# Second expert stage: 32 more tokens gathered instead of multiplied, v split and waited for in halves

## The reference, cut to what matters

```python
q = (xt @ w_query).reshape(n, PEER_HEADS, 2, PEER_DKEY // 2)
s = jnp.einsum('nhmd,mkd->nhmk', q, sub_keys).astype(jnp.float32)
sv, si = lax.top_k(s, PEER_TOPK)
...
fv, fpos = lax.top_k(cand, PEER_TOPK)
eidx = jnp.take_along_axis(cidx, fpos, axis=-1)
gate = jax.nn.softmax(fv, axis=-1).astype(h.dtype)
...
act = jax.nn.gelu(jnp.einsum('nd,nhkd->nhk', x_blk, expert_u[i_blk]))
return jnp.einsum('nhk,nhkd->nd', g_blk * act, expert_v[i_blk])
```

## Time and profile before

| | us |
|---|---|
| median of 3 runs | 4635.27 (4634.18 to 4642.76) |
| profiled execution | 4642.33, span 4640.6 |
| TensorE busy in the span | 4358.9 (94%) |
| second expert stage, first matmul to last add | 3298.1 to 4382.9 |
| TensorE busy in it (L2774) | 1074.2 for 6144 matmuls |
| mean granted TensorE clock | 0.971 |

### The profile page before, as it was taken

One profiled execution on the slowest core, in us unless ns is written; L12 is line 12 of the kernel. 1 busy time (PEld: TensorE's weight loads), 2 busy tenths in 40 slices (PEclk: granted clock), 3 DMA queues, 4 the chain that ended last, 5 costly groups with the idle time before them and its releaser, 6 DMA issues. The chain is left out here.

```text
span 4640.6 us, 80519 instructions
## 1 busy us (share of the span) xinstructions
PE 4358.9 (94%) x29764; PEld 4156.5 (90%) x29764; DVE 2641.2 (57%) x4339; ACT 1537.7 (33%) x2344; POOL 2535.1 (55%) x1826
## 2 busy tenths in 40 slices
PE   7899976999998898999999999999899999999999
PEld 5788875888787897999999999999899999999899
DVE  4477764554434302679566666655576767767621
ACT  3122213443443323223333333333333333333232
POOL 5687751322222342445566666657566666666543
PEclk9999987999999998999999999999899999999999
DMA  4233322334984532333589999979888888878533
GB/s 113 71 94 93 94 62 89 104 100 125 375 316 148 192 111 75 99 92 129 199 314 340 328 344 323 346 256 332 306 323 328 336 331 320 340 281 335 210 97 95
DMA packets 365052, 993.54 MB, mean 214 GB/s; under 512 B 43922, under 2 KB 121490, under 8 KB 305970
## 3 DMA queue, kind: packets, MB, share of 16 engines
q1 hardware_dynamic: 268370, 554.21, 36.1%
q0 software_dynamic: 46560, 337.14, 18.7%
q10 hardware_dynamic: 49920, 99.47, 5.6%
HBM read 904.93 MB, written 85.72 MB: 213 GB/s over the span
## 5 line engine op out<-in xcount | busy, mean ns | idle before, releaser
L2774 PE MATMUL val_y_ps<-val_wt,val_v 128*128 128x384 f32 x6144 | 1074.2, 335 | 30.4 <-DVE val_wt L2848 23.7
L2774 PEld LDWEIGHTS val_y_ps<-val_wt,val_v 128*128 128x128 f32 x6144 | 1068.0, 188 | 36.1 <-issue 31.4
L248 PE MATMUL rt_acc<-xn_act,rt_w_hi 128*128 128x384 f32 x4096 | 1062.8, 340 | 31.0 <-POOL rt_w_rest L238 30.7
L238 POOL TENSOR_TENSOR rt_w_rest<-rt_w_raw,rt_w_hi 128x512 fp32r<-128x512 f32 x576 | 736.9, 1304 | 509.5 <-ACT rt_w_hi L233 507.2
L248 PEld LDWEIGHTS rt_acc<-xn_act,rt_w_hi 128*128 128x128 f32 x4096 | 739.1, 188 | 46.3 <-POOL rt_w_rest L238 42.6
L2736 POOL TENSOR_TENSOR val_v<-val_v_raw,val_v 128x2048 fp32r<-128x2048 f32 x128 | 591.0, 4617 | 327.1 <-ACT val_v L2807 327.0
L248 PE MATMUL rt_acc<-xn_act,rt_w_rest 128*128 128x384 f32 x2048 | 691.8, 338 | 0.0
L2651 DVE CUSTOM_DVE_ANT_0 rt_space<-rt_space,rt_mid 128x2048 f32<-128x2048 f32 x160 | 360.9, 2280 | 216.1 <-DMA rt_space<-in_peer_u,out_row_id 208.5
L2869 DVE TENSOR_TENSOR out_xT<-out_xT,val_y_ps 128x384 f32<-128x384 f32 x512 | 282.3, 551 | 339.6 <-PE val_y_ps L2774 339.4
L233 ACT ACTIVATE rt_w_hi<-rt_w_raw 128x512 fp32r<-128x512 f32 x576 | 334.6, 627 | 283.3 <-PE rt_acc L248 196.7
L248 PEld LDWEIGHTS rt_acc<-xn_act,rt_w_rest 128*128 128x128 f32 x2048 | 383.7, 187 | 0.0
(11 more groups left out here) (428 smaller groups left out, 7308.8 us busy)
## 6 DMA issues: line engine op xcount, KB each, us to landing
rt_w_raw<-in_peer_uT SPq DMA_DIRECT2D x512, 256.0 KB, 5.2
val_v_raw<-in_peer_vp SPq DMA_DIRECT2D x128, 1024.0 KB, 5.0
scan_w_raw<-in_w_in SPq DMA_DIRECT2D x128, 256.0 KB, 3.2
att_w_raw<-in_w_in SPq DMA_DIRECT2D x96, 256.0 KB, 3.4
hid_scratch<-rt_hid ACTq DMA_DIRECT2D x128, 192.0 KB, 6.2
gate_scratch<-rt_space ACTq DMA_DIRECT2D x12, 2048.0 KB, 10.3
val_hid<-hid_scratch SPq DMA_DIRECT2D x32, 768.0 KB, 8.3
val_gate<-gate_scratch SPq DMA_DIRECT2D x32, 768.0 KB, 11.5
```

Source lines behind the costliest of these rows:

```text
L238: e.tensor_tensor(self.rest[:, s, 0:nk, :], self.raw[:, r, 0:nk, :], self.hi[:, s, 0:nk, :].bitcast(F32), ALU.subtract).then_inc(self.rest ...
L248: mm = e.matmul(acc[:, h, 0:width], w[:, s, k, :], act[:, kt0 + k, a, col + h * width:col + (h + 1) * width], start=first and k == 0 and w ...
L2774: mm = e.matmul(y_ps[:, t % 2, 0:DW], v[:, c % 2, a, j, t * P:(t + 1) * P], wt[:, g % 2, j, b, :], start=j == 0 and a == 0 and b == 0, sto ...
```

## The change

32 of the dense tokens, 160 to 191, become gathered tokens: `V0` = 192 is the first dense token of the second stage, `VTOK` = 352 their number, and 32 more gathers (`NV` = 192) bring their v rows. Their hidden values are still made by the dense product of the first stage; 32 single-element gathers (`picked`) fetch from `hid_scratch` what each of their picks needs. The gate table has 11 chunks. `v` and `v_rest` are handled in two halves of 256 columns: rounding, remainder and TensorE's wait are per half, and the gathers stand between the two remainders of a chunk. There are five row buffers, three turns of rows (`SETS`, `TURNS`), and the last set of rows ends one chunk ahead of the stage's end.

```diff
-ROWS, VROWS = 3, 4
+NV = NR + XK
+V0 = D0 + EX
+VTOK = TOK - V0
+ROWS, VROWS = 3, 5
...
-        NCH = DTOK // CH
+        NCH = VTOK // CH
...
             e.wait_ge(ids_ready, 1)
-            for g in range(P // EX):
-                r, c = slice(g * EX, (g + 1) * EX), slice(g * XK, (g + 1) * XK)
-                e.dma_start(k.row_id[r, HK:NR], more_id[:, c]).then_inc(more_in, 16)
-                e.dma_start(k.row_gate[r, HK:NR], more_gate[:, c]).then_inc(more_in, 16)
+            def spread(m):
+
+                picks, toks = slice(HK + m * XK, HK + (m + 1) * XK), slice(m * EX, (m + 1) * EX)
+                for g in range(P // EX):
+                    r, c = slice(g * EX, (g + 1) * EX), slice(g * XK, (g + 1) * XK)
+                    e.dma_start(k.row_id[r, picks], more_id[toks, c]).then_inc(more_in, 16)
+                    e.dma_start(k.row_gate[r, picks], more_gate[toks, c]).then_inc(more_in, 16)
+
+            spread(0)
             for u in range(2):
                 w.split_hi(e, 0, 0, base(FIRST_C) + u)
-            e.wait_ge(more_in, 2 * 16 * (P // EX))
+            spread(1)
+            e.wait_ge(more_in, 4 * 16 * (P // EX))
...
-        TURN = NG * HK // NR // 2 + 1
-        FIRST = 2 * TURN * NC
+        STARTS = (0, HK, NR)
+        TURNS = ((), (0, 1), (2,), (3, 4))
+        SETS = ((0, HK, 0, 84, 3), (HK, NR, 84, 108, 3), (NR, NV, 108, NG * NC, 1))
+        FIRST_PICK, GELU_PICKS, SCALE_PICKS = 8, 12, 14
 
         def rows_of(t):
 
-            n, last = FIRST - 3, NG * NC - FIRST
-            if t < FIRST:
-                return range(min(HK, -(-t * HK // n)), min(HK, -(-(t + 1) * HK // n)))
-            return range(HK - (-(t - FIRST) * XK // last), HK - (-(t + 1 - FIRST) * XK // last))
+            for a, b, first, last, spare in SETS:
+                if first <= t < last:
+                    lo, hi = (min(b, a - (-(x - first) * (b - a) // (last - first - spare))) for x in (t, t + 1))
+                    return range(lo, hi)
...
-                    e.wait_ge(v_rest, at(i, g, NC, c + 1))
+                    e.wait_ge(v_rest, at(i, g, 2 * NC, 2 * c + 2))
                     e.dma_start(v_raw[:, c % 2], k.peer_vp[ds(i * 2 + g, 1), c].rearrange("o p j n -> (o p) j n")
...
         @block.gpsimd
         def _(e):
-            e.sem_inc(v_rest, 2)
-
-            def split_rest(t):
-                e.wait_ge(v_hi, t + 1)
-                e.tensor_tensor(v[:, t % 2, 1], v_raw[:, t % 2], v[:, t % 2, 0].bitcast(F32),
-                                ALU.subtract).then_inc(v_rest, 1)
-
-            split_rest(0)
+            e.sem_inc(v_rest, 4)
+
+            def split_rest(t, hf):
+                e.wait_ge(v_hi, 2 * t + hf + 1)
+                e.tensor_tensor(v[:, t % 2, 1, :, side(hf)], v_raw[:, t % 2, :, side(hf)],
+                                v[:, t % 2, 0, :, side(hf)].bitcast(F32), ALU.subtract).then_inc(v_rest, 1)
+
             for t in range(NG * NC):
+                split_rest(t, 0)
+                if t == 0:
+                    split_rest(0, 1)
                 for n in rows_of(t):
                     if n >= VROWS:
                         e.wait_ge(row_done, n - VROWS + 1)
                     e.indirect_dma_start(rows[:, n % VROWS, :], None, k.peer_v,
                                          bass.IndirectOffsetOnAxis(ap=k.row_id[:, n:n + 1], axis=0)
                                          ).then_inc(rows_in[n % VROWS], 16)
+                n = t - FIRST_PICK
+                if 0 <= n < XK:
+                    e.wait_ge(hid_id_ready, 4)
+                    e.indirect_dma_start(picked[:, n:n + 1], None, hid_flat,
+                                         bass.IndirectOffsetOnAxis(ap=hid_id[:, n:n + 1], axis=0)
+                                         ).then_inc(picked_in, 16)
                 if t:
-                    split_rest(t)
+                    split_rest(t, 1)
...
-                    e.wait_ge(v_rest, at(i, g, NC, c + 3))
                     for t in range(CK):
+                        if t % 2 == 0:
+                            e.wait_ge(v_rest, at(i, g, 2 * NC, 2 * c + t // 2 + 5))
                         e.wait_ge(y_added, at(i, g, KT, c * CK + t + 1))
                         for j in range(GR):
                             for a, b in ((0, 0), (0, 1), (1, 0)):
-                                mm = e.matmul(y_ps[:, t % 2, 0:DW], v[:, c % 2, a, j, t * P:(t + 1) * P],
+                                mm = e.matmul(y_ps[:, t % 2, 0:VTOK], v[:, c % 2, a, j, t * P:(t + 1) * P],
...
             def split_v(i, g, c):
                 e.wait_ge(v_in[c % 2], at(i, g, 16 * NC // 2, 16 * (c // 2 + 1)))
-                e.wait_ge(y_ready, at(i, g, KT, c * CK + CK))
-                e.activation(v[:, c % 2, 0], v_raw[:, c % 2], ACT.Copy).then_inc(v_hi, 1)
+                for hf in range(2):
+                    e.wait_ge(y_ready, at(i, g, KT, c * CK + (hf + 1) * CK // 2))
+                    e.activation(v[:, c % 2, 0, :, side(hf)], v_raw[:, c % 2, :, side(hf)], ACT.Copy).then_inc(v_hi, 1)
...
+                if g == GELU_PICKS:
+                    e.wait_ge(picked_in, 16 * XK)
+                    e.activation(row_act[:, NR:NV], picked[:], ACT.Gelu_apprx_tanh).then_inc(row_gelu, 1)
...
-            e.wait_ge(row_done, NR)
-            e.wait_ge(row_turned, 4)
-            e.activation(row_out[:], row_ps[:], ACT.Copy).then_inc(row_out_done, 1)
+            e.wait_ge(row_done, NV)
+            e.activation(row_out[:, 2, :], row_ps[:], ACT.Copy).then_inc(row_out_done, 1)
...
+            e.tensor_tensor(lane_of[:], k.c("stack"), k.c("iota")[:, 0:EX], ALU.mult).then_inc(hid_id_ready, 1)
+            e.tensor_copy(hid_at[:], k.row_id[:, NR:NV]).then_inc(hid_id_ready, 1)
+            e.wait_ge(hid_id_ready, 2)
+            e.tensor_reduce(lane[:], lane_of[:], AX.X, ALU.add).then_inc(hid_id_ready, 1)
+            e.wait_ge(hid_id_ready, 3)
+            e.tensor_scalar(hid_id[:], hid_at[:], float(DTOK), lane[:], ALU.mult, ALU.add).then_inc(hid_id_ready, 1)
```

More of the change, by code:

```diff
@@ L2676, in stage_values @@
         rows = s.sb("rows", [P, VROWS, D_MODEL])
[L2677 to L2679 removed]
+        row_act = s.sb("row_act", [P, NV])
+        row_w = s.sb("row_w", [P, NV])
+        row_out = s.sb("row_out", [P, 3, D_MODEL])
+        hid_at = s.sb("hid_at", [P, XK])
+        hid_id = s.sb("hid_id", [P, XK], U32)
+        lane_of = s.sb("lane_of", [P, EX])
+        lane = s.sb("lane", [P, 1])
+        picked = s.sb("picked", [P, XK])
         v_raw = s.sb("v_raw", [P, 2, GR, VW])
         v = s.sb("v", [P, 2, 2, GR, VW], F32R)
[L2682 removed]
+        gate = s.sb("gate", [P, 2, VTOK // CH, GR, CH])
         hid = s.sb("hid", [P, 2, GR, DTOK])
[L2684 removed]
+        wt = s.sb("wt", [P, 2, GR, 2, VTOK], F32R)
         row_ps = s.ps("row_ps", [P, D_MODEL])
@@ L2752, in _, with turn @@
             e.sem_inc(y_ready, 2 * CK)
-            def turn(a):
-                if a >= 2:
-                    e.wait_ge(row_added, a - 1)
-                for t in range(4 * a, 4 * a + 4):
-                    mm = e.transpose(act_ps[:, a % 2, (t % 4) * P:(t % 4 + 1) * P], row_out[:, t * P:(t + 1) * P],
-                                     k.c("ident"))
+            def turn(m):
+                if m >= 2:
+                    e.wait_ge(row_added, m - 1)
+                if m in (2, 5):
+                    e.wait_ge(row_out_done, 2 if m == 2 else 3)
+                    for t in range(KT):
+                        mm = e.matmul(act_ps[:, m % 2, t * EX:(t + 1) * EX], row_out[:, 1 if m == 2 else 2, t * P:(t + 1) * P],
+                                      k.c("stack"), start=True, stop=True)
+                else:
+                    a = m if m < 2 else m - 1
+                    for t in range(4 * a, 4 * a + 4):
+                        mm = e.transpose(act_ps[:, m % 2, (t % 4) * P:(t % 4 + 1) * P], row_out[:, 0, t * P:(t + 1) * P],
+                                         k.c("ident"))
                 mm.then_inc(row_turned, 1)
@@ L2765, in part @@
                 for c in range(NC):
-                    if not more and c in (1, 3):
-                        turn(c - 1)
-                        turn(c)
-                    e.wait_ge(v_rest, at(i, g, NC, c + 3))
+                    if not more:
+                        for m in TURNS[c]:
+                            turn(m)
                     for t in range(CK):
+                        if t % 2 == 0:
+                            e.wait_ge(v_rest, at(i, g, 2 * NC, 2 * c + t // 2 + 5))
                         e.wait_ge(y_added, at(i, g, KT, c * CK + t + 1))
@@ L2784, in _ @@
             part(NG // 2 - 1, 1, False, False)
-            e.wait_ge(row_out_done, 2)
-            e.wait_ge(row_added, 4)
-            for t in range(KT):
-                mm = e.matmul(act_ps[:, 0, t * EX:(t + 1) * EX], row_out[:, t * P:(t + 1) * P], k.c("stack"),
-                              start=True, stop=True)
-            mm.then_inc(row_turned, 1)
+            turn(5)
```

(22 more changed lines are left out.)

65 lines of the change are left out of this document (32 added, 33 removed).

## The result

The changed kernel took 4666.04 us in the median of four runs (4662.99 to 4670.39), beside 4637.2 (4634.18 to 4642.76) for the kernel before, whose three runs a fourth had joined: a ratio of 1.0063, 95% interval 1.0051 to 1.0076. It is slower by 0.6%. The forecast was 4575, faster; the measured time lies above its whole range.

What follows compares the result with a forecast made beforehand. The prediction took TensorE to bound the stage of values. Its terms, -83.9 + 28 + 4 + 4.2 - 7.6 - 9.7 + 5.3 = -59.7, gave 4582.6 us, 4575 on the median's footing; forecast 4556 to 4596 (chance 0.51), whole range 4546 to 4618.

Steps and rivals of the forecast that it cites:

- Halves: Stage of values: splitting v into halves and moving the gathers between them shortens leads but costs nothing.
- The load of v: Stage of values: SP's load goes out later, lands in 5.0 us, leaves 3.1 us to spare; costed at nothing.
- The gather: Stage of values: rows issued 8.2 or 7.3 us ahead of use, landing in about 7; costed at nothing.
- Narrower matmuls: Stage of values: 352 columns instead of 384 save 13.65 ns on each of 6144 matmuls, -83.9 us; chunks last 7.66.
- The bytes: Stage of values: 384 MB instead of 352, at 390 GB/s, makes most chunks longer than 7.66 us: +28 us.
- VectorE: Stage of values: 19 chunks that close a group and have two rows delay `wt`, 9 before: +4 us.
- GpSimd: Stage of values: remainders, gathers and picks fit the period the bytes set anyway, so nothing is added.
- Turns: End of the stage of values: a third turn adds 4.2 us; an earlier last row and warm last turn save 7.6.
- Route stage: One of 12 gate chunks goes, with TensorE time and a twelfth of its waits: -9.7 us.
- the spread: Route stage: 8 DMA issues in ScalarE's queue delay its split and TensorE: +5.3 us, between 2 and 8.
- Late rows: Rival, stage of values: gathers land too late, VectorE and TensorE wait, about 4682 us, slower than before; chance 0.08.
- The two rivals of a lower DMA rate: Stage of values: DMA gives about 375 GB/s, 4610 us, chance 0.20; or 352 GB/s, about 4633 us, chance 0.06.

Runs made afterwards that it cites:

- e1: The changed kernel with each chunk's gathers and pick moved ahead of both halves' remainders on GpSimd: 4633.46 us, 0.9995 of the kernel before.
- e5: The changed kernel with both mends, a third v_raw buffer and the gathers ahead of both remainders: 4560.49 us, 0.9831 of the kernel before.
- e8: The changed kernel with three v_raw buffers, gathers ahead, picks in every second chunk and gathers of half a row: 4552.39 us, 0.9816 of before.

## Why the prediction was wrong

**The step that failed** is "Halves": "Nothing, then, but with less to spare than before." It saw both leads shrink and priced both at nothing, with the landing times that the trace of before shows. Two things were wrong in it.

*The load of v.* It put the load's landing at 5.0 us and found 3.1 to spare. What the change asks for is more bytes at once, and landing times answer to that. Issues of the changed kernel in the stage (KB each, median us from issue to landing):

```profile
val_v_raw<-in_peer_vp SPq DMA_DIRECT2D x126, 1024.0 KB, 7.5
...
val_gate<-gate_scratch SPq DMA_DIRECT2D x30, 704.0 KB, 15.2
val_rows<-in_peer_v,out_row_id POOLq DMA_INDIRECT x190, 7.9
```

With 7.5 in place of 5.0 the 3.1 us are down to 0.6, and the slowest load took 16.7 (10.0 before). The 3.1 were also the best case, one gather and no pick (1.10 us between the remainders): with two gathers and a pick, 3.60 us, they were 0.6 even at a landing of 5.0. The step laid out a chunk's times one by one and never closed the loop of a buffer, in which these 3.6 us count. Measured: 48 us for the third buffer alone. That the gathers' place is only part of it e1 shows: with them outside the loop ScalarE still waits 185.8 of 207.5 us for v.

*The gather.* It allowed 7 us of landing for a lead of 8.2 or 7.3. The median landing was 7.9, the lead where GpSimd itself ran late only 5.4. Measured: 33 us for the gathers ahead alone, 106 for both. That both bring more than 33 and 48 fits a reading in which the waits feed each other, late v making GpSimd late and with it the gather (the waits for rows fell from 80.2 to 60.7 us with the third buffer alone); no run shows it by itself.

Term by term, for the rest:

- **Narrower matmuls, -83.9**: right. A chunk takes 7.68 us where nothing is late, 7.66 was forecast.
- **The bytes, +28 at 390 GB/s**: the rate was right, the price was not. The kernel with both mends moves 393 GB/s over 3650 to 3900 us at a DMA share of 1.00 (375 at 0.95 over 3298 to 4300), and its chunks 40 to 80 take 7.83 us where 7.90 was forecast. That this is so near is luck: with half the rows' bytes they take 7.81. Over the whole stage half rows bring 10 us against e5 (1015.8 to 1006.0). In the changed kernel the share is 0.88, and late requests, not the rate, set the time. The Trainium skill (DMA: Bandwidth & Descriptors, Specifications) names about 358 GB/s of HBM per core; this core, alone at work, took 393 over 250 us, which is more, as the 405 in the earlier trace rows was.
- **VectorE, +4**: the right mechanism and count (19 later waits of TensorE for `wt` in e5), too small a price. A chunk that closes a group and has two rows lasts 0.66 us more than 7.68 in e5, 12 us for 18 of them; in the kernel before it is 0.45 more than 8.32, 4 us for 8. That is +8 where +4 was forecast.
- **GpSimd, 0**: right as a sum (817.7 of 1120 us busy), wrong as a place. The picks cost 11 us where they stood between the remainders; with both mends, spreading them took some 4 us off chunks 8 to 39.
- **Turns, +4.2 and -7.6**: right. The turn that came in took 3.88 us, the last 3.65 with no wait ahead of it, and what follows the last add is 7.2 us shorter:

```profile
4396.35 3.88 PE L2790 MATMUL val_act_ps<-all_const,val_row_out 128*128 128x32 f32 x32
...
4417.85 3.65 PE L2790 MATMUL val_act_ps<-all_const,val_row_out 128*128 128x32 f32 x32
```

- **Route stage, -9.7 and the spread, +5.3**: right within 2 us. The fp32 gate matmuls are busy 85.6 us, 7.8 less than in the earlier trace rows; the 1.9 us of waits did not go with them (36.1 us from 2200 to 3295 us, of which 13.7 at the spread; 29.9 before, of which 7.6). At the spread ScalarE's split starts at 2285.84 (2285.3 forecast), and TensorE waits 8.11 and 5.62 us where it waited 7.63, 6.1 more:

```profile
2276.01 1.01 PE L251 MATMUL rt_acc<-xn_act,rt_w_hi 128*128 128x384 f32 x2 [8.11 <-POOL rt_w_rest L241]
...
2287.88 1.01 PE L251 MATMUL rt_acc<-xn_act,rt_w_hi 128*128 128x384 f32 x2 [5.62 <-POOL rt_w_rest L241]
```

All of it ahead of the last stage came to -3.0, forecast -4.4. The kernel with both mends, in which the failed step is mended, took 4560.49 in the median, 15 under the 4575 forecast. Its stage took 1015.8 us, where the forecast's terms make 1037.0 (1084.7 - 83.9 + 28 + 4 + 4.2): the bytes were priced too high by more than VectorE was too low. By the starts of the chunks, the stage has 33 us above its pace in e5 and 20 in the kernel before; of the 13 more, VectorE makes 8 and the turn 4, so that about 1 is left for the bytes and all else. That 4560 lies in the forecast range is in part owed to two errors of opposite sign.

**The rivals.** "Late rows" was the one that ends slower, and its mechanism is half of what happened: VectorE stood for rows 60 times and TensorE behind it. Its threshold was wrong: it asked for a landing of 9.3 us against a mean lead of 7.7, and rows were late at a median of 7.9, because landings spread (5.4 to 13.3 us) and the lead was not 7.7 either. It got 0.08. Lateness of v, the larger half, was in no rival. Of the signs of being wrong that were named, the one of this rival came: chunks of 8.5 to 9.2 us with rows waiting for their landing. The two rivals of a lower DMA rate (375 and 352 GB/s) would have been read as confirmed by the changed kernel's 336 GB/s alone; the kernel with both mends refutes them. What is left in the stage with both mends is 33 us (1015.8 against 128 x 7.68 = 983). The starts of its chunks share them out: 12 in chunks that close a group and have two rows, 6 in the last four chunks, where the turns are, 4 in the first four, 4 in those with picks in mid-group, 3.5 in the first chunks of groups, 4 elsewhere. With half rows and spread picks (e8) 23 are left, the 12 and the 6 unchanged.

## What to carry to other kernels

When a change lets the bound engine run faster, close the loop of every buffer that feeds it (load, each step that uses it, whatever is queued between these steps, next load) and compare it with the new period times the number of buffers. Landing times of the old trace are those of the old load on the queues: allow for their growth, and for the spread, not the median. A low DMA rate beside waits for DMA may mean late requests; give the requests lead before calling it a ceiling. And busy DMA engines beside a chunk time near the forecast are no proof that bytes set it: take bytes away and see whether the chunk gets shorter.
